# VectorE makes the residuals of all weight slabs, GpSimd none; the slab rings and the stationary tiles start at multiples of 512 bytes

## The reference, cut to what matters

```python
def first_block(x, ...):
    xn = rmsnorm(h, norm_mix_g[l]);  u = xn @ w_in[l]            # 1024 x 7168
    q, k, v, xr, gr, ga, gb = jnp.split(u, splits, axis=-1)
    ya = chunked_band_attention(q, k, v, rel_table[l]) @ w_attn_out[l]
    xc = causal_depthwise_conv(xr, conv_w[l], conv_b[l])
    hr = rg_lru(xc, ...);  yb = (hr * jax.nn.gelu(gr)) @ w_rnn_out[l]
    h = h + (g_a * ya + g_b * yb) @ w_o[l]
    g, up = jnp.split(rmsnorm(h, norm_ffn_g[l]) @ w_ffn_in[l], 2, axis=-1)   # 1024 x 5632
    h = h + (jax.nn.silu(g) * up) @ w_ffn_out[l]                             # 2816 x 1024
def second_block(x, ...):
    h = h + 0.5 * rms_norm(swiglu(rms_norm(h, ffn1_pre_g), ffn1_w_gu, ffn1_w_down), ffn1_post_g)
    z = rms_norm(h, mix_pre_g) @ w_in                                        # 1024 x 1952
    mixed = concat([rms_norm(o_na), rms_norm(o_mla)]) @ w_out;  h = h + rms_norm(mixed, mix_post_g)
    h = h + 0.5 * rms_norm(swiglu(rms_norm(h, ffn2_pre_g), ffn2_w_gu, ffn2_w_down), ffn2_post_g)
```

## Time and profile before

| | us |
|---|---|
| median of 3 runs | 1010.09 |
| the runs | 1010.09, 2315.38, 1008.06 |
| the profiled execution, time | 1010.99 |
| its span in the profile | 1009.2 |
| PE busy | 964.2 |
| DVE busy | 500.5 |
| ACT busy | 491.2 |
| POOL busy | 356.6 |

### The profile page before, as it was taken

The page is one execution under the profiler, slowest core; times in us unless marked ns, Lnnn a source line. Parts: engine busy times, 40 slices in busy tenths (PEclk is TensorE's granted clock), DMA queues, the critical chain, the costliest instruction groups (busy, mean ns, idle before and its releaser), DMA issues.

```text
span 1009.2 us, 13878 instructions
## 1 busy us (share of the span) xinstructions
PE 964.2 (96%) x4535; PEld 792.5 (79%) x4535; DVE 500.5 (50%) x831; ACT 491.2 (49%) x771; POOL 356.6 (35%) x178
## 2 busy tenths in 40 slices
PE   5998979999999999999999999997999989999997
PEld 4877767888878888888878888876878868888886
DVE  3429595554445443342654433327478584334322
ACT  5353835664445444444544444436436464444442
POOL 4420000012434444354444444554512344343442
PEclk9999999999999999999999999999999999999999
DMA  6745453444545656779556565544612246555651
GB/s 216 232 161 167 126 185 122 125 143 144 173 162 175 194 173 190 249 221 240 168 175 193 174 191 183 188 151 148 195 43 84 84 129 205 188 186 186 184 184 72
DMA packets 133263, 169.27 MB, mean 168 GB/s; under 512 B 17723, under 2 KB 88926, under 8 KB 133094
## 3 DMA queue, kind: packets, MB, share of 16 engines
q1 hardware_dynamic: 132038, 168.67, 53.7%
q10 hardware_dynamic: 1184, 0.07, 0.1%
HBM read 167.61 MB, written 1.10 MB: 167 GB/s over the span
## 4 chain that ended last, share of the span: by engine, by line
PE 82%; DVE 10%; ACT 4%; issue 3%; DMA 1%; POOL 0%; DVEq 0%; ACTq 0%; POOLq 0%
PE acc L784 24%; PE acc L786 24%; PE acc L785 24%; PE tp L829 4%; DVE w_lo L1151 2%; DVE h L1522 1%; PE sc L902 1%; ACT w_hi L457 1%; PE acc L1088 1%; PE sc L1046 1%; DMA gain_x<-in_norm_mix_g 1%; DVE u L1237 1%; DVE xt_lo L1532 1%; DVE u L1201 0%; DVE u L1297 0%
## 5 line engine op out<-in xcount | busy, mean ns | idle before, releaser
L457 ACT ACTIVATE w_hi<-w_raw 128x1024 fp32r<-128x1024 f32 x305 | 322.0, 1059 | 386.8 <-PE acc L786 364.6
L1746 POOL TENSOR_TENSOR w_lo<-w_raw,w_hi 128x1024 fp32r<-128x1024 f32 x132 | 322.0, 2440 | 439.0 <-ACT w_hi L457 438.9
L1151 DVE TENSOR_TENSOR w_lo<-w_raw,w_hi 128x1024 fp32r<-128x1024 f32 x173 | 224.4, 1304 | 341.9 <-ACT w_hi L457 340.2
L784 PE MATMUL acc<-w_hi,xt_hi 128*128 128x512 f32 (+1 forms) x880 | 351.6, 399 | 4.6 <-DVE w_lo L1151 3.4
L786 PE MATMUL acc<-w_lo,xt_hi 128*128 128x512 f32 (+1 forms) x880 | 344.2, 391 | 0.0
L785 PE MATMUL acc<-w_hi,xt_lo 128*128 128x512 f32 (+1 forms) x880 | 343.7, 391 | 0.0
L784 PEld LDWEIGHTS acc<-w_hi,xt_hi 128*128 128x128 f32 x880 | 166.8, 190 | 39.9 <-DVE w_lo L1151 4.7
L786 PEld LDWEIGHTS acc<-w_lo,xt_hi 128*128 128x128 f32 x880 | 166.2, 189 | 35.1
L785 PEld LDWEIGHTS acc<-w_hi,xt_lo 128*128 128x128 f32 x880 | 166.7, 189 | 32.5
L784 PE MATMUL acc<-w_hi,hid_hi 128*128 128x512 f32 x264 | 105.0, 398 | 0.0
L785 PE MATMUL acc<-w_hi,hid_lo 128*128 128x512 f32 x264 | 104.6, 396 | 0.0
(11 more groups left out here) (192 smaller groups left out, 810.7 us busy)
## 6 DMA issues: line engine op xcount, KB each, us to landing
w_raw<-in_ffn_w_gu SPq DMA_DIRECT2D x176, 256.0 KB
w_raw<-in_w_in SPq DMA_DIRECT2D x68, 512.0 KB
w_raw<-in_w_ffn_in SPq DMA_DIRECT2D x88, 256.0 KB
w_raw<-in_ffn_w_down SPq DMA_DIRECT2D x44, 512.0 KB
w_raw<-in_w_ffn_out SPq DMA_DIRECT2D x22, 512.0 KB
w_raw<-in_w_rnn_out SPq DMA_DIRECT2D x8, 512.0 KB
w_raw<-in_w_attn_out SPq DMA_DIRECT2D x8, 512.0 KB
w_raw<-in_w_o SPq DMA_DIRECT2D x8, 512.0 KB
```

The source lines that it names most:

```text
L457: act.activation(w_hi[:, b, :], w_raw[:, b, :], ACT.Copy).then_inc(hi_done[b], 1)
L784: pe.matmul(o, hi[:, k, rows], wh, start=first and n == 0, stop=False)
L1151: dve.tensor_tensor(w_lo[:, b, :], w_raw[:, b, :], w_hi[:, b, :].bitcast(F32), ALU.subtract).then_inc(lo_done[b], 1)
L1746: pool.tensor_tensor(w_lo[:, b, :], w_raw[:, b, :], w_hi[:, b, :].bitcast(F32), ALU.subtract).then_inc(lo_done[b], 1)
```

## The change

DVE's `feed` makes the residual of every slab, POOL's `feed` and its calls are gone. In the loop over the groups of a feed-forward layer the last of a group's four slabs is fed behind the work of the group before (ACT's `tanhs`, DVE's `hidden`) and no longer ahead of it; that is so for ACT's `w_hi` and DVE's `w_lo`. At one place (`in2`) DVE's count goes from 1 to 2 for the same two slabs. `place` starts at 16896, rounds the start of tiles of 2048 bytes or more up to 64, and the tiles that share space start at a multiple of 512. That gives `w_raw` 16896, `xt_hi` 74240, `xt_lo` 82432, `hid_hi` 95744, `yt_hi` 153088 and `c_hi` 103936, all multiples of 512.

```diff
-    top = [16512]
+    top = [16896]
...
         if at is None:
+            if size >= 2048:
+                top[0] = (top[0] + 63) // 64 * 64
             at = top[0]
...
-    base = top[0]
+    base = top[0] = (top[0] + 511) // 512 * 512
...
-    def lo_on_dve(q):
-
-        return q % 2 == 0 or 20 <= q < 60
...
+                    feed(s_in + 4 * g + 6, 1, i, TURN)
                     tanhs(g, i)
+                    feed(s_in + 4 * g + 7, 1, i, TURN)
...
             def feed(s, n=1, i=0, turns=0):
 
                 for q in range(s, min(s + n, S["end"])):
-                    if lo_on_dve(q):
-                        b = q % RING
-                        wait(dve, hi_done[b], q // RING + 1, i, turns)
-                        dve.tensor_tensor(w_lo[:, b, :], w_raw[:, b, :], w_hi[:, b, :].bitcast(F32),
-                                          ALU.subtract).then_inc(lo_done[b], 1)
+                    b = q % RING
+                    wait(dve, hi_done[b], q // RING + 1, i, turns)
+                    dve.tensor_tensor(w_lo[:, b, :], w_raw[:, b, :], w_hi[:, b, :].bitcast(F32),
+                                      ALU.subtract).then_inc(lo_done[b], 1)
...
-                    feed(s_in + 4 * g + 6, 2, i, TURN)
+                    feed(s_in + 4 * g + 6, 1, i, TURN)
                     hidden(g, i)
+                    feed(s_in + 4 * g + 7, 1, i, TURN)
...
-                feed(S["in2"] + 2 * m, 1)
+                feed(S["in2"] + 2 * m, 2)
...
         @block.gpsimd
         def _(pool):
-            def feed(s, n=1, i=0, turns=0):
-
-                for q in range(s, min(s + n, S["end"])):
-                    if not lo_on_dve(q):
-                        b = q % RING
-                        wait(pool, hi_done[b], q // RING + 1, i, turns)
-                        pool.tensor_tensor(w_lo[:, b, :], w_raw[:, b, :], w_hi[:, b, :].bitcast(F32),
-                                           ALU.subtract).then_inc(lo_done[b], 1)
```

More of the change, by code:

```diff
@@ L1756, in _ @@
             pool.memset(q_stage[:], 0.0).then_inc(q_zero, 1)
-            feed(0, 4)
             pool.wait_ge(set_up, 1)
             rstd("x")
-            with pool.Fori(0, 2) as i:
-                feed(4, 8, i, 2)
             def stage(tile, group, i=0):
@@ L1780, in _ @@
                     stage(bass.ds(i * 4 + (2 * g + 2), 2), g + 1, i)
-            feed(60, S["f1i"] + 4 - 60)
             rstd("h1")
[L1783 to L1796, removed]
             rstd("h2")
-            feed(S["f2i"] + 4, 2)
             rstd("x2")
@@ L1806, in mask_head @@
                                    ALU.add).then_inc(bias2_ready, 1)
-            hidden(S["f2i"], S["f2o"], S["f2i"] + 6, mask_head)
+            for hd in range(8):
+                mask_head(hd)
             for m in range(MT):
                 rstd("f2", m)
-                feed(S["in2"] + 2 * m, 2)
             rstd("h3")
-            feed(S["in2"] + 4, 2)
-            feed(S["in2"] + 6, 4)
             rstd("q")
             rstd("kv")
-            feed(S["in2"] + 10, 9)
             for c in range(2):
@@ L1831, in _ @@
             pool.tensor_tensor(q2, rope[:, 2], rope[:, 3], ALU.add).then_inc(rope_q, 1)
-            feed(S["out2"], 4)
             rstd("na")
-            feed(S["out2"] + 4, 2)
             rstd("mla")
-            feed(S["out2"] + 6, 2)
             rstd("mix", 0)
-            feed(S["f3i"], 4)
             rstd("mix", 1)
             rstd("h4")
-            feed(S["f3i"] + 4, 2)
-            hidden(S["f3i"], S["f3o"], S["f3i"] + 6)
             for m in range(MT):
```

## The result

The changed kernel takes 1013.7 us (median of 12 executions) where the kernel before takes 1010.67: 1.0033 times as long, with a 95% interval of 1.0019 to 1.0047. It is slower by 3 us; the forecast was 7 faster. Its profiled execution is the slowest of the twelve (1016.09 us) and has a span of 1014.3 us.

What follows compares the result with a forecast made beforehand. The prediction took PE's matmul pace to bound the kernel, with stage edges where PE runs dry. Its terms, -7.2 and +0.05, sum to -7.15 us, giving 1003 us from a median of 1010.09; range 990 to 1013.

Steps and rivals of the forecast that it cites:

- The pace, -7.2: Matmuls with hid and yt stationary: starting at 64-byte multiples, 984 go from 234 to 226.7 ns, saving 7.2 us.
- Rival B: The 512-byte alignment also speeds up xt's matmuls; middle case 979 us, full case 954; chance 0.13.
- Rival C: The addresses do nothing; memory place or output-stage traffic sets the paces apart; 1010 us, chance 0.11.
- Part 2: POOL's residuals go to DVE; only edges between stages count, +0.05 us in all, bounds -4 to +14.8.
- The edges, +0.05: Sum over six edges between stages of residuals now in DVE's queue and blocking by POOL gone: +0.05 us.
- merge: Edge at 280 us: slab 75's residual stands ahead of adds PE waits for, less blocking gone: +0.35 us.
- h1: Edge at 307 us: slab 83's residual delays two adds, PE waits 0.9 us, splits add 0.3: +1.2 us.
- h2: Edge from 496 to 512 us: 0.9 us wait at first transposes, later blocking goes, two residuals come: -0.3 us.
- f2: Edge from 678 to 696 us: a second residual ahead of the first add_normed, both lose blocking: -1.4 us.
- softmax: Loop from 765 to 782 us, bound by DVE, which takes in slabs 231 and 233, less some blocking: +1.2 us.
- mix: Edge from 803 to 833 us: add_normed and coef lose blocking, one more residual stands ahead: -1.0 us.
- rival D: Slower: at the edges, residuals waiting for ACT's w_hi hold up work PE needs; 1018 us, chance 0.07.

Runs made afterwards that it cites:

- e7_stat: e3_bias with xt_hi and xt_lo at 32 behind a multiple of 64, hid, yt and c at 64 behind a multiple of 512: 1027.33 us.
- e10_both: e3_bias with other tile addresses: rings and xt at 160 behind a multiple of 512, hid at 416, yt at 288, c at 224: 1008.68 us.
- e3_bias: The changed kernel, with each of POOL's eight bias operations made to wait for w_hi of a slab of f2o: 1007.54 us.
- e4_before: The kernel before, run again unchanged to get the clock of each execution: 1010.2 us.
- e1_place: The kernel before with only the new addresses, residuals still split between DVE and POOL: 1005.66 us.
- e12_fill2: e3_bias with three residuals moved behind the drain or adds PE waits for, and PE's waits filled with unused transposes: 999.06 us.
- e2_dve: The changed kernel with the addresses of the kernel before, so only the residuals moved to DVE: 1018.95 us.

## Why the prediction was wrong

**The pace, -7.2.** Right in size: 7.0 by the stages. The reason was wrong. "What costs 7.3 ns is the half of 64 bytes" is refuted by `e7_stat` and `e10_both`; the distance to the moving operand decides, modulo 256 bytes. The prediction kept that distance as a side remark. It was luck that the size held: the change took `hid` and `yt` from a distance of 96 to 0, and a multiple of 64 alone does not give the pace (`e7_stat`, 64 from the rings, 233.3 ns). Rival B is gone with it: `xt` had distance 0 already, and stayed. Rival C is gone too. The rule of the Trainium skill (TensorE: Matmul & The Clock Gate, Part 2), that two independent ports keep the weight load from costing the running matmul anything, is not borne out: the paces differ with the distance of the two operands. What the two share is not shown.

**The step that failed** is in Part 2: what becomes of POOL's queue. I followed DVE's queue at every edge, and of POOL only its residuals, as something that goes; what stood behind them in its queue I put at nothing. A queue that is cleared lets what stood behind move up. The eight bias operations came 119 us earlier, next to DVE's work that PE waits for. That cost 5.8 us by the stages and 6.2 by the time of `e3_bias`. The Trainium skill (SBUF — State Buffer, SBUF: two separate sides) says that of DVE and GpSimd whichever starts first holds the shared ports for its whole instruction; the trace agrees (2.0 us for a residual beside a bias operation, 1.23 alone), but it tells nothing of when they meet.

**The edges, +0.05.** By `e3_bias` against `e4_before` and `e1_place`: merge +0.3 (forecast +0.35); h1 +1.8 (+1.2; the wait of 0.93 us was exact, the splits behind it were under-sized); h2 +0.55 (-0.3); f2 -1.2 (-1.4), softmax +0.9 (+1.2), mix -0.1 (-1.0), together about -0.35. Of the rows of h1 and h2, 0.2 and 0.4 us stand in `e1_place` too, where no residual moved. At the mix edge 2.1 us of PE's wait went, as forecast, and some 2.4 came with the wait for the residual that POOL used to make early; the prediction asked only what a residual holds back, not whether it comes late itself. And +1.15 at the end of the first loop, an edge that I had not on the list. In all +3.4. The check that was missing: every odd slab whose residual stood on POOL and whose `feed` on DVE is followed by work that PE waits for, not only the stages with a name.

**The clock.** I wrote that "a clock that falls at another edge than before would move 1 to 2 us". It is no matter of one: five of its 12 executions lie at 0.984, six of 99 of the kernel before at 0.986 or below. `e12_fill2` shows that filling PE's waits takes the falls away, and what they cost: 4.5 us even in the kernel with the short waits. Part of what the change lost at the edges it lost twice, as a wait and as the slower matmuls behind it. A faster PE also waits a little longer: at the merge 1.9 us in `e1_place` for 1.8 before, and 2.1 with the residual moved.

Together, by the stages: -7.0 + 3.4 + 5.8 = +2.2. Against the 1010.2 of `e4_before` 3.5 were measured; the other 1.3 us are not assigned. The clock at other places is the likely holder: the first row of the table has 2.4 us more after than in `e3_bias`, with four falls in place of one. Right were: the pace after, POOL without residuals, `add_normed` at 1.41 us for two, the gone wait for `h` at the mix edge, the wait of 0.9 us at 311 us, the order in the loops worth nothing. Wrong were 1003 and its range: rival D had the right sign and the wrong mechanism. The change as such is not bad: with one line more on POOL it is 2.7 us under the kernel before, with three residuals moved 6.7.

## What to carry to other kernels

When an engine is relieved, list what stands behind the removed work in its queue, and ask where it will run now and beside whom. When a product's two operands both come from SBUF, compare pace by pair of tiles, and place them a multiple of 256 bytes apart before aligning either (shown here for float32r and 512 columns). When a residual or the like changes its engine, ask two things at each edge: what it now holds back, and whether it still comes in time itself. Count a wait of TensorE of some 2 us for more than its length, since the clock may be at half behind it; filling it with work that nobody reads was worth 4.5 us here.

## What the runs showed of the hardware that was not expected

- Matmuls of 128x128 by 512 columns of float32r start 226.8 ns apart where the moving and the stationary tile lie a multiple of 256 bytes apart in SBUF, 232.6 to 232.8 at 128, 233.3 at 32 or 64, and 234.2 at 96. Absolute addresses (0, 128, 160, 224, 416 behind a multiple of 512) make no difference.
- The executions of one kernel differ in where the clock falls (at 96 us in the first trace of the kernel before, not in `e4_before`, behind the same wait of 2.7 us). Behind the wait of 3.8 us in the changed kernel it stayed at half for 6.8 us; in `e2_dve`, where that wait is as long, for 3.4.
- 13.4 ns remain between 226.7 and 213.3, which is half of the 426.7 ns at half clock and so an estimate for the bare columns. No pair of addresses tried came nearer; what they are is open.
